# Gated layer and projection behind the final norm: inputs split with a former scale, the ratio of scales put on the results in the banks

## What is computed

```python
h = h + peer(rmsnorm(h, g_ffn[i]), w_q[i], sub_keys[i], expert_u[i], expert_v[i])
gate = jax.nn.sigmoid(rmsnorm(h, g_ple[i]) @ w_pg[i])
h = h + (p[i] @ w_pe[i]) * gate
return rmsnorm(h, g_final)
...
u = h @ w_in        # s5_mixer, on rms_norm(x, ssm_norm), x being the line above's result
```

## Time and profile before

| | us |
|---|---|
| median of 3 runs (lowest, highest) | 3038.6 (3038.53, 3046.92) |
| the profiled execution, own time | 3039.05 |
| its span | 3037.3 |
| PE busy | 2655.0 (87%) |
| DVE busy | 1975.5 (65%) |
| POOL busy | 1686.7 (56%) |
| ACT busy | 808.9 (27%) |
| chain that ended last: POOL's queue, DMA, PE, issue, DVE | 28%, 25%, 19%, 17%, 7% |

### The profile page before, as it was taken

One profiled execution on the slowest core, in us unless ns is written; L12 is line 12 of the kernel. 1 busy time (PEld: TensorE's weight loads), 2 busy tenths in 40 slices (PEclk: granted clock), 3 DMA queues, 4 the chain that ended last, 5 costly groups with the idle time before them and its releaser, 6 DMA issues.

```text
span 3037.3 us, 32275 instructions
## 1 busy us (share of the span) xinstructions
PE 2655.0 (87%) x9712; PEld 1223.6 (40%) x9827; DVE 1975.5 (65%) x3886; ACT 808.9 (27%) x1755; POOL 1686.7 (56%) x1018
## 2 busy tenths in 40 slices
PE   7889888888888878887787879999999977999999
PEld 3344333333333333333333754444444434444444
DVE  7847777777777777777778763666244675466523
ACT  2332222222222222222233331222122255222101
POOL 5544444444444444444355947777776620677776
PEclk9999999999999999999988879999999997999999
DMA  4249999999999999999932213233332300233332
GB/s 138 64 175 421 422 421 414 416 417 415 412 415 412 417 417 412 408 413 419 406 123 72 70 45 99 96 104 106 110 100 77 123 31 1 83 98 104 116 102 80
DMA packets 133096, 696.13 MB, mean 229 GB/s; under 512 B 29867, under 2 KB 31180, under 8 KB 67052
## 3 DMA queue, kind: packets, MB, share of 16 engines
q0 software_dynamic: 73728, 536.90, 42.9%
q1 hardware_dynamic: 59244, 157.74, 16.0%
HBM read 686.72 MB, written 7.86 MB: 229 GB/s over the span
## 4 chain that ended last, share of the span: by engine, by line
POOLq 28%; DMA 25%; PE 19%; issue 17%; DVE 7%; POOL 2%; ACT 1%; DVEq 1%; SPq 0%; ACTq 0%
DMA R<-expert_uv_dram,idx 25%; POOLq L2484 13%; POOLq L2482 12%; PE bank L531 10%; PE bank L755 8%; DVE R L1967 3%; POOLq L2526 1%; POOL R L2509 1%; POOLq L2524 1%; DVE Z L1989 1%; ACT Z L1309 1%; POOL R L2520 1%; DVE ci L1913 0%; DVE R L1979 0%; DVE R L1914 0%
## 5 line engine op out<-in xcount | busy, mean ns | idle before, releaser
L755 PE MATMUL bank<-R,Z 128*128 128x512 f32 x2048 | 972.7, 620 | 231.0 <-ACT Z L1309 226.3
L531 PE MATMUL bank<-R 128*128 128x512 f16 (+1 forms) x4471 | 1006.2, 383 | 38.7 <-DVE R L1696 10.8
L2509 POOL DMA_INDIRECT R<-expert_uv_dram,idx x512 | 596.8, 1166 | 721.5 <-PE bank L755 669.9
L2481 POOL TENSOR_TENSOR R<-wring,beat 128x1024 f16<-128x1024 f32 (+2 forms) x226 | 461.4, 2042 | 557.4 <-PE bank L531 509.7
L1967 DVE SCALAR_TENSOR_TENSOR R<-R 128x1024 f32<-128x1024 f32 x512 | 623.5, 1222 | 207.8 <-DMA R<-expert_uv_dram,idx 206.2
L755 PEld LDWEIGHTS bank<-R,Z 128*128 128x128 f32 x2048 | 383.0, 195 | 804.9 <-issue 419.1
L531 PEld LDWEIGHTS bank<-R 128*128 128x128 f16 x4560 | 442.9, 98 | 598.3 <-issue 41.3
L2483 POOL TENSOR_TENSOR R<-wring,R 128x1024 bf16<-128x1024 f32 (+2 forms) x226 | 524.5, 2321 | 40.4 <-issue 7.5
L1309 ACT ACTIVATE Z<-consts,R 128x128 f32<-128x128 f32 x512 | 177.7, 394 | 321.6 <-DVE R L1979 321.6
L531 PE MATMUL bank<-Z,R 128*128 128x512 f16 (+1 forms) x1082 | 238.8, 379 | 2.7 <-POOLq L2484 1.5
L1302 ACT ACTIVATE R<-R 128x2 f32<-128x2 f32 x256 | 52.1, 204 | 618.6 <-DVEq L1969 618.2
(11 more groups left out here) (325 smaller groups left out, 2430.0 us busy)
## 6 DMA issues: line engine op xcount, KB each, us to landing
wring<-up_dram SPq DMA_DIRECT2D x88, 512.0 KB, 3.5
wring<-down_dram SPq DMA_DIRECT2D x32, 704.0 KB, 4.1
wring<-ple_dram SPq DMA_DIRECT2D x16, 640.0 KB, 3.9
wring<-w_in_dram SPq DMA_DIRECT2D x18, 512.0 KB, 3.5
R<-expert_uv_dram,idx POOLq DMA_INDIRECT x512, 12.3
wring<-glu_dram SPq DMA_DIRECT2D x16, 512.0 KB, 3.6
Z<-w_q_dram SPq DMA_DIRECT2D x11, 512.0 KB, 8.1
wring<-ple_a_dram SPq DMA_DIRECT2D x8, 640.0 KB, 6.2
```

The lines of the kernel that those rows point to most:

```text
L531: mm = pe.matmul(bank[:, :], low(w) if i else w, low(v) if j else v, start=(start and c == 0 and p == 0), stop=(stop and c == n - 1 and p ...
L755: mm = pe.matmul(banks[2 * par + c][:, :], diag[:, k % 4, :], pairs[:, slot, 1, c * SEQ:(c + 1) * SEQ], start=(k == 0), stop=(k == TOPK - 1))
L2481: po.tensor_tensor(wsp[:, slot, 0, 0:w], src, one.broadcast_to([P, w]), ALU.mult)
L2509: po.indirect_dma_start(pairs[:, slot, :, :].rearrange("p a b -> p (a b)"), None, A["expert_uv"], bass.IndirectOffsetOnAxis(idx[:, n % 2, ...
```

## The change

**Former scale.** The reciprocal root of the lookup's own norm (`old_inv`, with `old_root`) is kept. In the last head, DVE multiplies the finished token tiles of `hT` by it (`old_scaled`, one 128x1024 TENSOR_TENSOR for each of token tiles 0 to 2, two of 128x512 for tile 3, from `hT` and the bank `scale_bank` into Z), ACT writes gain times that as the high part into `XO` (`old_high`, 8 of 128x128 for each token tile), DVE the low part (`old_low`, 8 of 128x128). PE spreads `old_inv` once in unit 30 and once more in the gated layer.

**Gated layer.** It now takes the other form: PE starts on `XO` as its tiles come (5 feature tiles, row means, 3 feature tiles, spread), and the scale `inv * old_root` is put on each gate bank by `scale_tile`. The split of `p` on DVE (`p_low`) moves behind `old_low`. The barrier at the lookup's end is gone for PE, ACT and DVE.

**Projection.** While the gated layer runs, each finished tile of `hT` is multiplied by both gains and `old_inv` into `stat_bank` (`final_tile`), ACT copies the high part, DVE takes the low part (`final_low`). PE multiplies slab 0 with them, then sums the squares, multiplies slabs 1 and 2, spreads both scales, and goes on; the scale `inv * inv2 * old_root` is put on each of the 8 results (`scaled`) before ACT moves it on. The 8 multiplies of `hT` move into the stage `ssm`.

**POOL** does one 128x1 operation and a drain behind its last gather (`tick`), its first four slabs of the gated layer are no longer in a loop, and slab 1 no longer waits for PE (`w_used`).

```diff
@@ PE
+            def spread_old():
+
+                for j in range(NT):
+                    mm = pe.matmul(scale_bank[:, j * P:(j + 1) * P], ident[0:NT, j:j + 1].broadcast_to([NT, P]), old_inv,
+                                   start=True, stop=True)
+                mm.then_inc(old_spread, 1)
...
+                    if name == "ple_a" and u == 0:
+                        pe.wait_ge(s_ready, S_READY["ple_a"])
+                        spread_old()
...
-                pe.wait_ge(ss_ready, NORM["final_a"] + 1)
-                row_means(sumsq, stat_bank)
-                row_means(sumsq2, tile_banks[1])
-                norm_spread(NORM["ssm_in"], inv_both, scale_bank)
-                norm_spread(NORM["ssm_in"], inv, stat_bank)
                 finished(pe)
...
+                for u in range(SLABS["ssm_in"]):
+                    pe.wait_ge(split_done, used(s0 + u))
+                    free_bank(t0 + u, 0, 0)
+                    product(banks[(t0 + u) % NBANK], (s0 + u) % NSPLIT, 0, KT, xs, None if u else gn_ready, G0["ssm_in"])\
+                        .then_inc(mm_done, 1)
+                    if u == 0:
+                        pe.wait_ge(ss_ready, NORM["final_a"] + 1)
+                        row_means(sumsq, stat_bank)
+                        row_means(sumsq2, tile_banks[1])
+                    if u == 2:
+                        norm_spread(NORM["ssm_in"], inv_both, scale_bank)
+                        norm_spread(NORM["ssm_in"], inv, stat_bank)
@@ ACT
+                def old_high(T):
+                    ac.wait_ge(old_ready, T + 1)
+                    for k in range(KT):
+                        if T == NT - 1 and k == NT:
+                            ac.wait_ge(old_ready, T + 2)
+                        ac.activation(XO[:, k, 0, T * P:(T + 1) * P], old_tile[:, k, :], ACT.Copy, scale=col("g_ple", k))\
+                          .then_inc(gn_hi if T == NT - 1 else old_hi, 1)
...
+                        if then == "final_a":
+                            ac.wait_ge(xn_ready, KT + n + 1)
+                            ac.activation(xs[:, n, 0, :], stat_bank[:, :], ACT.Copy).then_inc(gn_hi, 1)
...
+                ac.wait_ge(rb_mm, NORM["final_a"] + 1)
+                ac.activation(S_row, scale_bank[:, :], ACT.Copy).then_inc(s_ready, 1)
@@ DVE
+                def old_scaled(T):
+
+                    ts = slice(T * P, (T + 1) * P)
+                    ve.wait_ge(old_spread, 1)
+                    ve.drain()
+                    for ks in (slice(0, NT), slice(NT, KT)) if T == NT - 1 else (slice(0, KT),):
+                        ve.tensor_tensor(old_tile[:, ks, :], hT[:, ks, ts],
+                                         scale_bank[:, ts].unsqueeze(1).broadcast_to([P, ks.stop - ks.start, P]), ALU.mult)\
+                          .then_inc(old_ready, 1)
...
                     stream_add(T)
+                    old_scaled(T)
+                    old_low(T)
+                    p_low("ple_a")
                     ve.wait_ge(last_sq, 2)
                     stream_sum(T)
...
+            def final_low(n):
+
+                ve.wait_ge(gn_hi, G0["ssm_in"] + n + 1)
+                ve.tensor_tensor(low(xs[:, n, 1, :]), stat_bank[:, :], xs[:, n, 0, :], ALU.subtract).then_inc(gn_ready, 1)
+
+            def final_tile(n):
+
+                if n:
+                    final_low(n - 1)
+                else:
+                    ve.wait_ge(old_spread, 2)
+                ve.drain()
+                ve.scalar_tensor_tensor(stat_bank[:, :], hT[:, n, :], both_gains[:, n:n + 1], scale_bank[:, :],
+                                        ALU.mult, ALU.mult).then_inc(xn_ready, 1)
...
             if stage("ssm_in"):
-                ve.wait_ge(rb_mm, NORM["final_a"] + 1)
-                norm_tiles("ssm_in", lambda k: both_gains[:, k:k + 1], xs, a_ready)
-                ve.wait_ge(rb_mm, NORM["ssm_in"] + 1)
-                for k in range(KT):
-                    ve.scalar_tensor_tensor(hT[:, k, :], hT[:, k, :], col("g_final", k), stat_bank[:, :],
-                                            ALU.mult, ALU.mult)
...
+                ve.wait_ge(s_ready, S_READY["ssm_in"])
+                scaled(0, 1, 2)
                 ve.wait_ge(prep, 3)
                 mul(AR, AR, bigM)
...
@@ POOL
-                    if not (isinstance(r, int) and s - NSPLIT < FIRST):
+                    if not (isinstance(r, int) and (s - NSPLIT < FIRST or s == SLAB0["ple_a"] + 1)):
                         po.wait_ge(w_used, r * NSLOT + used(s - NSPLIT + 1))
...
+                tick()
                 po.wait_ge(diag_done, UNITS * TOPK)
```

More of the change, by code:

```diff
@@ L593, in plain @@
                         product(banks[u], u % NSPLIT, 0, kt, x, ready if u == 0 else None, base).then_inc(mm_done, 1)
[L595 to L604, removed]
-                        if u == 0:
-                            pe.wait_ge(p_split, PLES.index(name) + 1)
-                        product(banks[(2 * u + 1) % NBANK], u % NSPLIT, KT, 2, ps_a if name == "ple_a" else ps,
-                                first_of_slab=False).then_inc(mm_done, 1)
             def halves(name, x, ready, base):
@@ L1157, in norm_root @@
                 ac.wait_ge(stat_mm, i + 1)
-                ac.activation(root, stat_bank[0:NT, 0:P], ACT.Sqrt, bias=eps[0:NT, :]).then_inc(rs_ready, 1)
+                ac.activation(old_root if i == NORM["peer"] else root, stat_bank[0:NT, 0:P], ACT.Sqrt, bias=eps[0:NT, :]).then_inc(rs_ready, 1)
             def high_parts(name, parts):
@@ L1322, in head @@
                             diags(n, T % 2, i)
+                            if last and (T, i) in OLD_AT:
+                                old_high(OLD_AT[T, i])
                             if i == 0 and T == 2 and h == 0:
@@ L2010, in stream_sum, with old_low @@
                     ve.tensor_reduce(sumsq[:, T * P:(T + 1) * P], hsq.rearrange("p k t -> p t k"), AX, ALU.add)
+                def old_scaled(T):
[6 more added lines that the diff above has]
+                          .then_inc(old_ready, 1)
+                def old_low(T):
+                    ts = slice(T * P, (T + 1) * P)
+                    ve.drain()
+                    for k in range(KT):
+                        if T == NT - 1:
+                            ve.wait_ge(gn_hi, G0["ple_a"] + k + 1)
+                        else:
+                            ve.wait_ge(old_hi, T * KT + k + 1)
+                        part = ve.scalar_tensor_tensor(low(XO[:, k, 1, ts]), old_tile[:, k, :], col("g_ple", k),
+                                                       XO[:, k, 0, ts], ALU.mult, ALU.subtract)
+                        if T == NT - 1:
+                            part.then_inc(gn_ready, 1)
                 def into_stream(T):
                     stream_add(T)
+                    old_scaled(T)
+                    old_low(T)
+                    p_low("ple_a")
                     ve.wait_ge(last_sq, 2)
@@ L2033, in unit @@
                     weigh(n, par, 2)
+                    if finished and T == 2:
+                        old_scaled(0)
                     if top_next:
@@ L2039, in unit @@
                     weigh(n, par, 3)
+                    if finished and T == 2:
+                        old_low(0)
                     dots(n, par, T, 4)
@@ L2160, in gated @@
                         gain_low(then, KT - 1)
+                    if then == "final_a":
+                        final_low(KT - 1)
             def ple(name, gains, then):
-                if name in GAINS:
-                    norm_scale(NORM[name])
-                    ve.wait_ge(s_ready, S_READY[name])
-                else:
-                    norm_apply(name, gains)
+                norm_scale(NORM[name])
+                ve.wait_ge(s_ready, S_READY[name])
                 gated(name, 0, then)
```

115 lines of the change are left out of this document (72 added, 43 removed).

## The result

The changed kernel takes 3055.4 us (median of 6 runs, 3053.2 to 3057.8), the kernel before 3039.3 beside it: a ratio of 1.0045, 95% interval 1.0033 to 1.0057. It is 16 us slower by the medians (14 by the ratio, 10 to 17 by its interval), where 3 were forecast, and lies above the range's top of 3049.0. From here on, differences are those of the medians; the ratio with its interval, always against the kernel before run beside it, says how firm they are.

What follows compares the result with a forecast made beforehand. The bound was taken to be when DVE has the tables' powers ready, carried by POOL through the recurrence: 1618.5 + 47.5 = 1666.0 against 1663.0, +3 us, so a median of 3041.5 us, range 3033.5 to 3049.

Steps and rivals of the forecast that it cites:

- POOL then carries that time through the recurrence: Recurrence: only when DVE has the tables' powers ready (1663.0 before) counts; POOL, busy 97 of 107 us, passes it on.
- the powers' +3: End of the projection's opening: the tables' powers ready at 1666.0 against 1663.0, so +3 us for the kernel.
- the recurrence's length changes: Recurrence: one of the signs listed beforehand that would show the prediction wrong; no size was given.
- anything else: Whole kernel: outcomes outside the forecast and its rivals, chance 0.04, spread over both sides.
- Lookup additions at nothing: Lookup's last two units: DVE's added multiplies and low parts, 10 us together, hide behind gathers; 0 to 2 us if not.
- POOL's stall gone: POOL's first slabs: the 7.36 us stall before slab 0's second pass vanishes; slab 0 ends at 1529.3, slab 1 at 1534.4.
- rival (a): POOL's first slabs: the 7.36 us stall stays, slab 0 ends at 1536.4; +10, in all 3048.5 us; chance 0.12.
- S = 1550.5: Gated layer's opening: scale row ready at 1550.5, range 1544.4 to 1552.2; last tile's low parts end at 1540.9, colliding with POOL.
- Gated layer S + 68: Gated layer: DVE becomes the bound at 5.64 us a tile plus 20 us of table steps, through at 1618.5; costs 14 us.
- rival (b): Gated layer: DVE keeps up with PE, table steps falling into POOL's pauses; powers at 1654.5, 3026.5 to 3030 us; chance 0.08.
- ACT's table loads: Ahead of the gated layer's first sigmoid: two table loads on ACT, 1.28 us each by the rows, not about 2.66.
- From there to the powers 47.5 us: Projection, from DVE's end of the gated layer to the powers: 47.5 us against 58.6 before, a gain of 11 us.

Runs made afterwards that it cites:

- e1: The kernel before with two extra 128x1024 products and a drain each on DVE just ahead of the powers, a pure delay; 3054.1 us, ratio 1.0036.
- e3: The changed kernel with ten extra 128x128 products of constants per recurrence step on PE, into a bank nobody reads (a filler); 3035.0 us, ratio 0.9983.
- e9: The whole change with fillers (idle PE products) in the recurrence, behind it and in the first slab of `glu`, and in the attention; 3032.0 us, ratio 0.9966.
- e12: The kernel before with fillers (idle PE products) in the recurrence, behind it and in the first slab of `glu`, and in the attention; 3029.2 us, ratio 0.9955.
- e2: The kernel before with only the gated layer's half of the change, final norm and projection as before; 3034.8 us, ratio 0.9978.
- e6: The kernel before with only the gated layer's half of the change, plus the recurrence filler of ten idle PE products per step; 3032.9 us, ratio 0.997.
- e7: The kernel before with only the gated layer's half of the change, plus idle PE products in recurrence, opening of `glu` and attention; 3028.0 us, ratio 0.995.
- e5: The kernel before with ten idle 128x128 PE products per recurrence step, nothing else changed; 3037.9 us, ratio 0.999.

## Why the prediction was wrong

The step that failed is the last one, "POOL then carries that time through the recurrence", and with it the sum, which added to the powers' +3 a rest taken as fixed. That rest was 1374.2 us long before and 1388.0 after. The prediction had the sign in hand: the earlier trace rows shows the recurrence at a granted clock of 0.89, and it named "the recurrence's length changes" as what would make it wrong, but it gave that no case and no price, and no chance beyond the 0.04 for anything else. In the place of a fixed rest the runs showed three stretches whose length follows the granted clock: 14 us for a delay of 2.6 (e1), 20 us back for idle products on PE (e3), and the same rest in both kernels with all fillers (e9, e12). Step by step, up to there:

- **Lookup additions at nothing:** right. hT is whole at 1532.26 (before 1532.56).
- **POOL's stall gone:** right; rival (a) is refuted. Slab 0 ended at 1531.3 instead of the forecast 1529.3, because it started 2.1 us later than before, on its weights' DMA. Slab 2 came at 1548.96, not near 1535.5: it needs slab 1's first matmul, which I had counted one slab too early. The miss cost nothing.
- **S = 1550.5:** 1546.6, the scale row's end. The low parts of the last tile took 4.54 us, against 2.19 in the tiles inside the lookup, and ended at 1538.3, between the two cases (1536.2 and 1540.9). By the Trainium skill's rule (SBUF — State Buffer, Who interferes with whom) they contend with POOL; the trace agrees, as far as 2.35 us of waiting beside POOL's second pass show it. But the pass was slab 1's (1533.90 to 1536.56), not slab 2's as forecast: had that pass ended at 1534.4, as forecast, little would have collided, so that they waited at all is luck. Of the 3.9 us that S came early, 2.5 are that shorter wait (the sum of squares ended at 1541.6, not 1544.1), and 1.3 are PE: its row means took 1.04 us and its spread 1.15, at a granted clock of 1.00, where I had taken values between the levels.
- **Gated layer S + 68:** S + 71.6. The tile itself is exact (5.65 us from 1575.41 to 1581.06, forecast 5.64). The table steps and what stands between the tiles took 22.8 us (1553.81 to 1616.12, less seven tiles) instead of 20: one step took 3.63 us beside POOL, another (L2167) 1.22. The last low part and squares took 2.1 instead of 1.2. DVE was the bound as forecast, PE waited four times, 15.0 us in all; rival (b) is refuted. The two errors, -3.9 and +3.6, cancelled by luck: 1618.2 against 1618.5.
- **ACT's table loads:** 1.28 us each here too, as the rows said. The Trainium skill (ScalarE: Activation LUTs, What ACT_TABLE_LOAD costs) has about 1.28 us for the load and 1.38 for a drain, 2.66 together. Here, too, only the load's part was seen, with the next operation 0.02 us behind it.
- **From there to the powers 47.5 us:** 48.1; powers' first matrix at 1666.29 for 1666.0. DVE's wait ahead of the first scale multiply was 2.1 us, not 5.

So +3 at the powers was met, in part by errors that cancelled, and e9 against e12 gives +2.7 for the whole. What was missing is the clock: about 13 of the 16 us.

Kernels with the same code up to the powers reach them up to 2.3 us apart in their profiles (1659.0, 1658.7 and 1656.7 in e2, e6 and e7; 1666.3 and 1664.5 after and in e9; 1661.9 and 1663.7 in e5 and e12), so single traces size these steps, and the +3 with them, no finer. What decides in a given execution whether the clock falls at a pause isn't settled: the kernel before had pauses of 1.50 and 1.49 us at the place where the changed kernel had 1.55 and 1.89. Nor is it settled what makes the opening of `glu` take 116 to 121 us in ten traces and 127 to 131 in four. Why e7's recurrence begins at the low level until 1690 is open too.

## What to carry to other kernels

Where a stretch has a granted clock below 1.00 in its windows, its length isn't a constant of the sum: give it a case of its own, priced from rows at both levels, before adding a delay ahead of it. A pure delay in the kernel before, and products of constants in TensorE's pauses, tell in two runs whether a lost gain is the clock's; compare medians of several executions there, not one trace with another. And keep the fillers where they bring the time down: here some 200 products without any use are worth 12 us to the kernel before (e12, 3029.2 against 3041.0 beside it), more than the better half of the change (5 us, e2).

## What the hardware showed that was not expected

- A delay of 2.6 us ahead of the recurrence cost 14 us (5 to 16 by its interval), and one of 5.2 us cost 10 (4 to 11).
- The granted clock fell to 0.50 in the midst of a stretch in which PE was busy 16.7 of the 20 us ahead (1702 to 1722), with no pause longer than 1.89 us in them, and stayed there some 20 us although PE then was full (10.00 of 10 us busy from 1725 to 1735).
- The spread of one kernel's times goes with the clock as well. e1's twelve executions lie between 3036.7 and 3060.5 us, with mean clocks from 0.952 to 0.961; e7's six, with all fillers, between 3024.1 and 3030.0, with 0.968 to 0.974.
